# A decoder layer on one core: the squares of two norms summed by VectorE instead of TensorE, and the low parts of two tiles ahead of the samples

## The chip, the cores and the metric

One Trainium2 chip, one of its cores. The metric is the device time of one execution in microseconds (us), lower is better. The times of the kernel before are 2039.47, 2039.68 and 2043.07 us, median 2039.68.

## What is computed

One inference step of a hybrid decoder layer for 256 prompt tokens and 8 samples of 4 tokens, 288 columns in all, in float32, model width 2048. The parts that the change touches are the norm between the two sub-layers and the final norm:

```python
def _rmsnorm(x, g):
    xf = x.astype(jnp.float32)
    y = xf * lax.rsqrt(jnp.mean(xf * xf, axis=-1, keepdims=True) + NORM_EPS)
    return (y * g.astype(jnp.float32)).astype(x.dtype)
...
    x = x + gt1 * jnp.dot(mix, p["w_o"])

    h2 = _rmsnorm(x, p["g_norm2"]) * (1.0 + sc2) + sh2
    u, ffn_buf_new = _causal_dwconv(jnp.dot(h2, p["w_up"]), ffn_buf, p["w_ffn_conv"])
    u_gate, u_val = jnp.split(u + p["b_ffn_conv"], 2, axis=-1)
    x = x + gt2 * jnp.dot(jax.nn.silu(u_gate) * u_val, p["w_down"])
...
    y_prompt = _rmsnorm(h_p, g_final)
    y_sample = _rmsnorm(h_s, g_final)
```

## The kernel before

Everything is kept feature-major: x is 16 tiles (KT) of 128 features by 288 columns (256 of the prompt, SEQ, then 32 of the samples, NS). The weights come from memory as one stream of slots of 512 KB, each four tiles of input features (KS) by two tiles of output features (CT), into eight buffers raw_a and on. For float32 accuracy each slot is split: ScalarE rounds it into a high part (L740, hi_a to hi_c, a ring of four), GpSimd subtracts to get the rest (L700, written beside or over the raw slot). TensorE then does 24 matmuls of 288 columns for a slot: for each of 4 x 2 weight tiles high x high (L2150), high x low of the activation (L2151), and behind them, when the rest is there, rest x high (L2155). The names hi, lo and rest are these parts.

The order of the work on every engine is written out by hand; engines wait for each other through counters (semaphores), and each engine executes its own list in order.

A product runs in groups: a group is one pair of output tiles, 4 slots in the w_o product (phase "wo", 8 groups, three sets of two PSUM banks) and 3 slots in the last of three down products (phase "dn2", 8 groups, two sets of banks). Behind each group VectorE adds the gated result to two tiles of x (residual, L2003 to L2010) and raises x_done or down_done; ScalarE squares the two tiles into the two halves of sq (squares_of, L751), for which it waits until sq_used says that the halves are free. It does that at places in its own list between weight conversions. TensorE sums a square over the 128 features of a tile with a matmul against a matrix of ones into bank 7 (norm_part, L2182). The profile shows each such float32 matmul as two. In the w_o product the sums of group g-1 are issued behind group g; in the last down product behind the second slot of group m (the hook within=). The sums of the last pair follow alone, in both norms, and then norm_end raises ssq_ready; ScalarE turns bank 7 into the reciprocal root (rms, L757 and L759).

After the norm in the middle, second_norm on VectorE and tiles_round on ScalarE produce h tile by tile. For the prompt columns of tile k VectorE scales x into a bank (L1371), ScalarE rounds it into h_hi (L789), and VectorE forms the low part h_lo (second_lo, L1356), two tiles later in its list. The sample columns go in two bunches, tiles 0 to 3 (ka) and 4 to 15 (kb): scaled and shifted by VectorE (second_samples, L1343 and L1346), rounded by ScalarE (L787), low part by VectorE (second_lo_samples, L1351). TensorE's first group of the up product waits for the low part of each tile in turn, and for the low samples of ka before its first slot and of kb before its second. The change in the diff's second part moves the calls for kb within second_norm's loop over k.

After the last norm VectorE scales all 16 tiles of x (L2092), and the output is stored.

Of the kernel before, what the change touches and what calls it, by code (L numbers as in the profile page):

```python
# [17 lines left out]
P = 128  # L18
# [8 lines left out]
N = SEQ + NS  # L27
NC = 1 + DB
NCP = NC + NC % 2
KT = D_MODEL // P  # L30
KS, CT = 4, 2
# [128 lines left out]
SUPERS = ((0, 4), (4, 4), (8, 3))  # L160
# [88 lines left out]
def decoder_step(nc, A, O):  # L249
    f32, f32r, i32 = mybir.dt.float32, mybir.dt.float32r, mybir.dt.int32  # L250
    ALU, ACT, AX = mybir.AluOpType, mybir.ActivationFunctionType, mybir.AxisListType
    ds = bass.ds
    ctx = ExitStack()
    with ctx:
# [23 lines left out]
        ident, ones = cv["ident"], cv["ones"]  # L278
# [103 lines left out]
        np_ = Place(rows_at)  # L382
        sq = np_.take("sq", [P, 2, N])
        ht_at = np_.at
        hs = Place(ht_at).take("hs", [P, KT, NS])
        np_.at += 4 * HB * N
        hf = np_.take("hf", [P, HB, SEQ])
        amul = np_.take("amul", [P, KT, NC])

# [73 lines left out]
        bank = [ctx.enter_context(nc.psum_tensor(f"bank{i}", [P, 512], f32)) for i in range(8)]  # L463
# [3 lines left out]
        def sem(name):  # L467
            return ctx.enter_context(nc.semaphore(name))
# [13 lines left out]
        sq_ready, sq_used, ssq_ready, rs_ready = sem("sq_ready"), sem("sq_used"), sem("ssq_ready"), sem("rs_ready")  # L482
        xr_ready, sq_sum = sem("xr_ready"), sem("sq_sum")
# [35 lines left out]
        def grp(name, sets, g, i=0, per=0):  # L519

            return g % sets, gbase[name][g % sets] + g // sets + i * (per // sets)
# [9 lines left out]
        def raw_at(name, j, i=0, per=0):  # L531

            s_ = BASE[name] + j
            first, _, size, before = next(t for t in stretches if t[0] <= s_ < t[1])
            return (s_ - first) % size, before[(s_ - first) % size] + (s_ - first) // size + i * (per // size)

        def wait_group(eng, name, g, i=0, per=0):

            if name == "go":
                j, per_j = 2 * g + 1, 2 * per  # L540
            elif name[:2] == "dn":
                k = SUPERS[int(name[2])][1]
                j, per_j = k * g + k - 1, k * per
            else:
                j, per_j = 4 * g + 3, 4 * per
            r, use = raw_at(name, j, i, per_j)
            eng.wait_ge(raw_free[r], use + 2)
# [693 lines left out]
        def _(dve):  # L1241
            V = nc.vector
            T_, S_, STT, CP = V.tensor_tensor, V.tensor_scalar, V.scalar_tensor_tensor, V.tensor_copy
# [97 lines left out]
            def second_samples(ks, count):  # L1341

                T_(hs_p[:, ks, :], hs[:, ks, :], bank[7][:, SEQ:N].unsqueeze(1).to_broadcast([P, count, NS]), ALU.mult)  # L1343
                dve.drain()
                sh = ada[:, 3 * KT + ks.start:3 * KT + ks.stop, 1:NC].unsqueeze(2).to_broadcast([P, count, TS, DB])
                T_(tb16(hs_p[:, ks, :]), tb16(hs_p[:, ks, :]), sh, ALU.add).then_inc(hs_t, 1)  # L1346

            def second_lo_samples(ks, n):

                dve.wait_ge(hs_hi, n)  # L1350
                T_(h_lo[:, ks, SEQ:], hs_p[:, ks, :], h_hi[:, ks, SEQ:].bitcast(f32), ALU.subtract).then_inc(hs_lo, 1)  # L1351
# [7 lines left out]
            def second_norm():  # L1359

                ka, kb = slice(0, 4), slice(4, KT)
                T_(tb16(hs[:, :, :]), tb16(x[:, :, SEQ:]), of_b16(amul[:, :, 1:NC]), ALU.mult)
                dve.drain()
                dve.wait_ge(rs_ready, 2)
                second_samples(ka, 4)
                for k in range(KT):
                    if k >= 2:
                        second_lo(k - 2)
                    if k >= 3:
                        dve.wait_ge(h_lo_ready, KT + HB + k - 2)  # L1370
                    STT(bank[4 + k % 3][:, 0:SEQ], x[:, k, 0:SEQ], amul[:, k, 0:1], bank[7][:, 0:SEQ], ALU.mult, ALU.mult).then_inc(h_t, 1)  # L1371
                    if k == 1:
                        second_lo_samples(ka, 5)
                        second_samples(kb, KT - 4)
                    if k == 3:
                        second_lo_samples(kb, 6)
                second_lo(KT - 2)
                second_lo(KT - 1)
# [68 lines left out]
            def iqm_half(u):  # L1447
# [3 lines left out]
                for same in (1, 0):  # L1451
# [7 lines left out]
            sets = [(sc_p[:, 0:P], wk_p[:, 0:P], top8[:, 0, :]), (sc_p[:, P:], wk_p[:, P:], top8[:, 1, :]),  # L1459
                    (sc_s[:, :], wk_s[:, :], top8[:, 2, :])]  # L1460
# [537 lines left out]
            def residual(bs, t, gate_tile):  # L1998
# [11 lines left out]
                    T_(xt[:, SEQ:], xt[:, SEQ:], bank[2 * bs + c][:, SEQ:N], ALU.add)  # L2010
                dve.drain()

            dve.wait_ge(hist_in, 16)
            h_old, h_new = hcx[:, :, 0:DB], hcx[:, :, DB:HI_F]
            wf = lambda w_: vec[:, V_WF + w_ * 2 * FT:V_WF + (w_ + 1) * 2 * FT].unsqueeze(2).to_broadcast([P, 2 * FT, DB])
# [5 lines left out]
            second_scale()  # L2021
            for g in range(KT // CT):
                bs, _ = grp("wo", 3, g)
                wait_group(dve, "wo", g)
                if g % (KT // CT // 2) == 0:
                    dve.wait_ge(x_back[g // (KT // CT // 2)], 16)
                residual(bs, 2 * g, 2 * KT)
                dve.sem_inc(grp_free[bs], 1)
                dve.sem_inc(x_done, 2)
# [48 lines left out]
            for n, (first, count) in enumerate(SUPERS):  # L2078
                with dve.Fori(0, count) as i:
                    for half in range(2):  # L2080
                        up_pair(f"up{n}", half, first, i)
                for m in range(KT // CT):
                    bs, _ = grp(f"dn{n}", 2, m)
                    wait_group(dve, f"dn{n}", m)
                    residual(bs, 2 * m, 5 * KT)
                    dve.sem_inc(grp_free[bs], 1)
                    dve.sem_inc(down_done, 1)
# [8 lines left out]
        def _(pe):  # L2096
            MM = nc.tensor.matmul
# [60 lines left out]
                            ins.then_inc(ring_free, 1)  # L2158
                ins.then_inc(raw_free[r], 1)

            def group(name, sets, g, j0, nslots, hi_t, lo_t, i=0, per_g=0, per_j=0, norm=None, chunk=None, mixed=False, within=None):

                bs, cnt = grp(name, sets, g, i, per_g)
                banks = (bank[2 * bs], bank[2 * bs + 1])
                pe.wait_ge(grp_free[bs], cnt + 1)
                for s_ in range(nslots):
                    if norm is not None and s_ < 2:
                        pe.wait_ge(hs_lo, 5 + s_)
                    if mixed:
                        pe.wait_ge(mix_done, 2 * s_ + 2)  # L2170
                    if chunk is not None:
                        pe.wait_ge(act_ready, 2 * (chunk + s_) + 2)
                    slot(name, j0 + s_, lambda k: hi_t(s_ * KS + k), lambda k: lo_t(s_ * KS + k), banks,
                         s_ == 0, s_ == nslots - 1, i, per_j, None if norm is None else norm * KT + HB + s_ * KS)
                    if within is not None and s_ == 1:
                        within()

            hh, hl = (lambda k: h_hi[:, k, :]), (lambda k: h_lo[:, k, :])

            def norm_part(n, s_):  # L2180
                pe.wait_ge(sq_ready, 4 + (n - 1) * KT + s_ + 1)
                MM(bank[7][:, 0:N], ones, sq[:, s_ % 2, :], start=(s_ == 0), stop=(s_ == KT - 1)).then_inc(sq_used, 1)  # L2182

            def norm_end(n):
                pe.wait_ge(sq_used, n * KT + 2)
# [435 lines left out]

            for g in range(KT // CT):
                group("wo", 3, g, 4 * g, 4, mh, ml, mixed=g == 0)
                for s_ in range(CT * g - CT, CT * g):
                    if s_ >= 0:
                        norm_part(1, s_)
            for s_ in range(KT - CT, KT):
                norm_part(1, s_)
            norm_end(1)
# [1 line left out]
            ah, al = (lambda k: act_hi[:, k, :]), (lambda k: act_lo[:, k, :])  # L2631
            for n, (first, count) in enumerate(SUPERS):
                up, dn = f"up{n}", f"dn{n}"
                if n == 0:
                    for g in range(4):
                        group(up, 2, g, 4 * g, 4, hh, hl, norm=None if g else 1)
                peel = 1 if n == 0 else 0
                with pe.Fori(0, count - peel) as i:
                    for g in range(4):
                        group(up, 2, g + 4 * peel, 4 * g + 16 * peel, 4, hh, hl, i, 4, 16)  # L2640
                if n < len(SUPERS) - 1:
                    with pe.Fori(0, KT // CT // 2) as i:
                        for m in range(2):
                            group(dn, 2, m, count * m, count, ah, al, i, 2, 2 * count, chunk=first)
                else:
                    for m in range(KT // CT):
                        def sums(m=m):
                            for s_ in range(CT * m - CT, CT * m):
                                norm_part(2, s_)
                        group(dn, 2, m, count * m, count, ah, al, chunk=first, within=sums if m else None)  # L2650
            for s_ in range(KT - CT, KT):
                norm_part(2, s_)
            norm_end(2)
# [112 lines left out]
```

## Time and profile before

| | |
|---|---|
| median of three runs | 2039.68 us (2039.47 to 2043.07) |
| the profiled execution, its own time | 2045.23 us |
| its span | 2043.4 us |
| w_o product with its norm sums | about 1071 to 1169 us of the span |
| h of the second norm, TensorE at half clock | about 1172 to 1182 |
| three up and down products | 1175 to 2027.5 |
| last down product with its norm sums | about 1944 to 2031 |
| last scaling and store | 2033 to the end |

The profile is one execution. Its page gives busy times and the span in 40 slices; the views of the trace used below are the busy time of each engine in chosen windows with the granted clock of TensorE (1.00 is 2.4 GHz, 0.50 is 1.2 GHz), the chain of work that ended last in order of time, the timeline of one engine, and the instructions of one tile. Matmuls overlap: one of 288 columns shows as 0.29 us, but they start 0.13 us apart, so starts are what is to be compared.

### The profile page before, as it was taken

What the parts mean: (1) busy time and instruction counts of PE and PEld (TensorE: products, weight loads), DVE (VectorE), ACT (ScalarE), POOL (GpSimd) and SP (SyncE); (2) the same over time, 40 slices, a digit from 0 to 9 for tenths busy, and PEclk for the clock granted to TensorE, in tenths of its full rate; (3) what the DMA queues carried; (4) which work ended last, traced back from release to release, by engine and by line L of the source; (5) the groups of instructions that cost most, each with busy time, mean ns of one, the idle gap of its engine ahead of it and who ended that gap; (6) DMA issues with size and microseconds to landing.
All of it is one profiled execution on the core that took longest, in us unless ns stands there. A gap on an engine that the chain in (4) does not pass through costs nothing.

```text
span 2043.4 us, 38282 instructions
## 1 busy us (share of the span) xinstructions
PE 1957.9 (96%) x15132; PEld 1835.6 (90%) x15132; DVE 619.1 (30%) x1722; ACT 827.2 (40%) x1365; POOL 1179.4 (58%) x496
## 2 busy tenths in 40 slices
PE   6899989999989989999899899999999999999997
PEld 2399989998878878888799899999999999999996
DVE  1347534443214233232251142221122221122212
ACT  1353436643214232242443455553344443344432
POOL 0176646663424334333587667777777777777763
PEclk9699999999999999999999999999999999999998
DMA  9966434444868877888874444444544445444442
GB/s 393 411 213 196 136 104 142 149 163 126 227 206 245 251 238 232 248 244 247 260 224 159 138 144 166 164 164 165 164 166 165 167 166 168 166 165 165 164 161 77
DMA packets 177856, 390.77 MB, mean 191 GB/s; under 512 B 27522, under 2 KB 101698, under 8 KB 177090
## 3 DMA queue, kind: packets, MB, share of 16 engines
q1 hardware_dynamic: 156592, 370.11, 55.6%
q10 hardware_dynamic: 21138, 18.90, 2.9%
q8 instruction: 89, 1.46, 0.3%
q14 instruction: 37, 0.30, 0.0%
HBM read 380.01 MB, written 8.88 MB: 190 GB/s over the span
## 4 chain that ended last, share of the span: by engine, by line
PE 87%; DMA 7%; ACT 2%; DVE 2%; issue 1%; DVEq 0%; ACTq 0%; POOL 0%; SPq 0%; PEldq 0%; POOLq 0%
PE bank L2150 25%; PE bank L2151 25%; PE bank L2155 24%; DMA raw_a<-in_stream 4%; PE bank L2126 2%; DMA raw_c<-in_stream 1%; PE bank L2487 1%; PE bank L2495 1%; PE bank L2498 1%; DMA raw_b<-in_stream 1%; PE bank L2591 1%; PE bank L2182 1%; PE bank L2570 1%; PE bank L2102 1%; PE bank L2115 1%
## 5 line engine op out<-in xcount | busy, mean ns | idle before, releaser
L700 POOL TENSOR_TENSOR rest_a<-raw_a,hi_a 128x1024 fp32r<-128x1024 f32 x185 | 442.5, 2394 | 460.5 <-ACT hi_a L740 460.5
L2150 PE MATMUL bank<-h_hi,hi_a 128*128 128x288 f32 x1752 | 488.1, 304 | 6.7 <-ACT hi_a L740 5.6
L2151 PE MATMUL bank<-h_lo,hi_a 128*128 128x288 f32 x1752 | 477.0, 298 | 0.0
L2150 PEld LDWEIGHTS bank<-h_hi,hi_a 128*128 128x128 f32 x1752 | 334.2, 191 | 23.1 <-issue 13.7
L740 ACT ACTIVATE hi_a<-raw_a 128x1024 fp32r<-128x1024 f32 x185 | 195.9, 1059 | 371.0 <-PE bank L2155 230.8
L2151 PEld LDWEIGHTS bank<-h_lo,hi_a 128*128 128x128 f32 x1752 | 334.9, 191 | 0.4
L2155 PE MATMUL bank<-h_hi,rest_a 128*128 128x288 f32 x1600 | 245.6, 296 | 0.1
L2155 PEld LDWEIGHTS bank<-h_hi,rest_a 128*128 128x128 f32 x1600 | 224.8, 190 | 0.3 <-POOL rest_a L700 0.3
L700 POOL TENSOR_TENSOR rest_b<-raw_b,hi_a 128x1024 fp32r<-128x1024 f32 x67 | 161.4, 2409 | 100.5 <-ACT hi_a L740 100.5
L700 POOL TENSOR_TENSOR rest_a<-raw_a,hi_b 128x1024 fp32r<-128x1024 f32 x56 | 134.6, 2404 | 64.6 <-ACT hi_b L740 64.6
L2150 PE MATMUL bank<-h_hi,hi_b 128*128 128x288 f32 x616 | 167.9, 299 | 0.0
L2151 PE MATMUL bank<-h_lo,hi_b 128*128 128x288 f32 x616 | 165.6, 295 | 0.0
L740 ACT ACTIVATE hi_a<-raw_b 128x1024 fp32r<-128x1024 f32 x67 | 70.9, 1059 | 140.2 <-PE bank L2155 102.4
L2003 DVE SCALAR_TENSOR_TENSOR x<-bank,ada,x 128x256 f32<-128x256 f32 x64 | 28.0, 480 | 316.9 <-PE bank L2155 316.7
L700 POOL TENSOR_TENSOR rest_b<-raw_b,hi_c 128x1024 fp32r<-128x1024 f32 x39 | 93.5, 2397 | 45.9 <-ACT hi_c L740 45.9
L2150 PEld LDWEIGHTS bank<-h_hi,hi_b 128*128 128x128 f32 x616 | 115.6, 188 | 0.8 <-ACT hi_a L740 0.3
L2151 PEld LDWEIGHTS bank<-h_lo,hi_b 128*128 128x128 f32 x616 | 116.0, 188 | 0.3
L700 POOL TENSOR_TENSOR rest_a<-raw_a,hi_c 128x1024 fp32r<-128x1024 f32 x39 | 93.4, 2396 | 35.2 <-ACT hi_c L740 35.2
L700 POOL TENSOR_TENSOR rest_c<-raw_c,hi_a 128x1024 fp32r<-128x1024 f32 x39 | 94.0, 2410 | 31.3 <-ACT hi_a L740 31.2
L700 POOL TENSOR_TENSOR rest_c<-raw_c,hi_b 128x1024 fp32r<-128x1024 f32 x39 | 93.8, 2406 | 29.9 <-ACT hi_b L740 29.9
L2155 PE MATMUL bank<-h_hi,rest_b 128*128 128x288 f32 x696 | 106.7, 296 | 0.1
L740 ACT ACTIVATE hi_b<-raw_a 128x1024 fp32r<-128x1024 f32 x56 | 59.4, 1060 | 110.1 <-PE bank L2155 108.9
(486 smaller groups left out, 3960.2 us busy)
## 6 DMA issues: line engine op xcount, KB each, us to landing
raw_a<-in_stream SPq DMA_DIRECT2D x396, 512.0 KB, 3.7
raw_b<-in_stream SPq DMA_DIRECT2D x160, 512.0 KB, 3.3
raw_c<-in_stream SPq DMA_DIRECT2D x94, 512.0 KB, 3.3
raw_m<-in_stream SPq DMA_DIRECT2D x34, 512.0 KB, 6.5
st<-in_state ACTq DMA_DIRECT2D x16, 512.0 KB, 7.0
out_state_s<-st ACTq DMA_DIRECT2D x8, 512.0 KB, 6.3
x<-in_x SPq DMA_DIRECT2D x2, 1152.0 KB, 13.7
x<-in_x ACTq DMA_DIRECT2D x2, 1152.0 KB, 6.6
```

The source lines that it names most:

```text
L700: nc.gpsimd.tensor_tensor(rest_in(name, r), raw_of(name, r), w_hi[q].bitcast(f32), ALU.subtract).then_inc(lo_ready, 1)
L740: A_(w_hi[q], raw_of(name, r), ACT.Copy).then_inc(hi_ready, 1)
L2003: STT(xt[:, 0:SEQ], bank[2 * bs + c][:, 0:SEQ], gt[:, 0:1], xt[:, 0:SEQ], ALU.mult, ALU.add)
L2102: return nc.tensor.transpose(out, in_, ident[0:n, 0:n])
L2115: last = MM(bank[2 * (n % 2)][32 * k:32 * k + NCP, 0:CT * P], c_f[:, s_ * KS + k, :], raw[r][:, k, :], start=(s_ == 0), stop=(s_ == KT // ...
L2126: last = MM(bank[2][32 * q:32 * q + NCP, 0:CT * P], c_f[:, k, :], raw_m[r][:, q, :], start=(k == 0), stop=(k == KT - 1))
L2150: MM(banks[c][:, 0:N], w_, hi_of(k), start=(first and k == 0), stop=False)
L2151: ins = MM(banks[c][:, 0:N], w_, lo_of(k), start=False, stop=False)
L2155: ins = MM(banks[c][:, 0:N], rest_in(name, r)[:, k, c * P:(c + 1) * P], hi_of(k), start=False, stop=(last_ and k == KS - 1))
L2182: MM(bank[7][:, 0:N], ones, sq[:, s_ % 2, :], start=(s_ == 0), stop=(s_ == KT - 1)).then_inc(sq_used, 1)
L2487: ins = MM(blk(3, ch), bt[:, l % 2, ch, :], tt[:, 4 + ch, :], start=True, stop=True)
L2495: ins = MM(blk(4, ch), x_p[:, ch, :], tt[:, ch, :], start=True, stop=True)
```

## The change

Seven of the eight pairs of squares in each of the two norms are no longer summed by TensorE one by one. VectorE copies the first pair (two tiles, 128x576) into a new buffer sq_acc and adds the next six to it, each ahead of the residual of the following group, and raises sq_used itself. TensorE sums the two halves of sq_acc with two matmuls behind the last group, and the last pair as before. The hook within= goes. sq_acc lies over a buffer (hf) that only the first norm uses.

In second_norm the samples of tiles 4 to 15 are scaled after k = 3 instead of after k = 1, and their low part comes after k = 5 instead of after k = 3. The low parts of tiles 0 and 1 are thereby ahead of them in VectorE's list.

```diff
+        sq_acc = Place(np_.at).take("sq_acc", [P, 2, N])
         hf = np_.take("hf", [P, HB, SEQ])
...
                     if k == 1:
                         second_lo_samples(ka, 5)
+                    if k == 3:
                         second_samples(kb, KT - 4)
-                    if k == 3:
+                    if k == 5:
                         second_lo_samples(kb, 6)
...
+            def gather_squares(n, g):
+
+                dve.wait_ge(sq_ready, 4 + (n - 1) * KT + 2 * g + 2)
+                if g == 0:
+                    CP(sq_acc[:, :, :], sq[:, :, :]).then_inc(sq_sum, 1)
+                else:
+                    dve.wait_ge(sq_sum, 4 + (n - 1) * (KT // CT - 1) + g)
+                    T_(sq_acc[:, :, :], sq_acc[:, :, :], sq[:, :, :], ALU.add).then_inc(sq_sum, 1)
+                dve.wait_ge(sq_sum, 4 + (n - 1) * (KT // CT - 1) + g + 1)
+                dve.sem_inc(sq_used, 2)
...
             for g in range(KT // CT):
                 bs, _ = grp("wo", 3, g)
+                if g:
+                    gather_squares(1, g - 1)
                 wait_group(dve, "wo", g)
...
                     bs, _ = grp(f"dn{n}", 2, m)
+                    if n == len(SUPERS) - 1 and m:
+                        gather_squares(2, m - 1)
                     wait_group(dve, f"dn{n}", m)
...
-                    if within is not None and s_ == 1:
-                        within()
...
-                MM(bank[7][:, 0:N], ones, sq[:, s_ % 2, :], start=(s_ == 0), stop=(s_ == KT - 1)).then_inc(sq_used, 1)
+                MM(bank[7][:, 0:N], ones, sq[:, s_ % 2, :], start=False, stop=(s_ == KT - 1)).then_inc(sq_used, 1)
+
+            def gathered_part(n):
+
+                pe.wait_ge(sq_sum, 4 + n * (KT // CT - 1))
+                for c in range(2):
+                    MM(bank[7][:, 0:N], ones, sq_acc[:, c, :], start=(c == 0), stop=False)
...
                 group("wo", 3, g, 4 * g, 4, mh, ml, mixed=g == 0)
-                for s_ in range(CT * g - CT, CT * g):
-                    if s_ >= 0:
-                        norm_part(1, s_)
+            gathered_part(1)
             for s_ in range(KT - CT, KT):
                 norm_part(1, s_)
...
-                        def sums(m=m):
-                            for s_ in range(CT * m - CT, CT * m):
-                                norm_part(2, s_)
-                        group(dn, 2, m, count * m, count, ah, al, chunk=first, within=sums if m else None)
+                        group(dn, 2, m, count * m, count, ah, al, chunk=first)
+            gathered_part(2)
             for s_ in range(KT - CT, KT):
                 norm_part(2, s_)
```

## Rows read from the trace of the kernel before

**Rows 1.** The page: busy us of each engine; TensorE's clock in 40 slices.
```profile
PE 1957.9 (96%) x15132; PEld 1835.6 (90%) x15132; DVE 619.1 (30%) x1722; ACT 827.2 (40%) x1365; POOL 1179.4 (58%) x496
...
PEclk9699999999999999999999999999999999999998
```

**Rows 2.** Windows: length, busy us (instructions) by engine, clock, DMA share, GB/s.
```profile
1100.00:1165.00 65.00, 65.00 (x479) 64.16 (x478) 5.46 (x24) 25.06 (x31) 45.21 (x20) 1.00 0.46 155
...
1954.00:2027.00 73.00, 73.00 (x530) 71.52 (x529) 9.48 (x42) 24.50 (x33) 42.68 (x18) 1.00 0.34 113
```

**Rows 3.** The chain in the w_o product: start us, length us, what.
```profile
1083.82 0.97 PE bank L2182 x4
...
1100.60 1.07 PE bank L2155 x8
1103.79 1.07 PE bank L2155 x8
...
1152.29 0.97 PE bank L2182 x4
```

**Rows 4.** The same chain in the last down product.
```profile
2002.35 0.97 PE bank L2182 x4
...
2023.38 0.97 PE bank L2182 x4
```

**Rows 5.** Timeline at both norms' ends: start, length, engine, line, operation [idle before].
```profile
1165.82 1.13 PE L2182 MATMUL bank<-sq,consts 128*128 128x288 f32 x4
1168.11 1.24 PE L2182 MATMUL bank<-sq,consts 128*128 128x288 f32 x4 [1.16 <-ACT sq L751]
...
2029.68 1.24 PE L2182 MATMUL bank<-sq,consts 128*128 128x288 f32 x4 [2.14 <-ACT sq L751]
...
1153.92 0.78 ACT L751 ACTIVATE sq<-x 128x288 f32<-128x288 f32 x2 [1.39 <-DVEq L2028]
...
1167.61 0.78 ACT L751 ACTIVATE sq<-x 128x288 f32<-128x288 f32 x2 [4.57 <-DVEq L2028]
```

**Rows 6.** Timeline after norm 1: TensorE, VectorE, ScalarE.
```profile
1175.01 0.58 PE L2150 MATMUL bank<-h_hi,hi_c 128*128 128x288 f32 x1 [5.66 <-DVE h_lo L1356]
...
1177.97 0.61 PE L2150 MATMUL bank<-h_hi,hi_c 128*128 128x288 f32 x1 [0.70 <-DVE h_lo L1356]
...
1180.06 2.12 PE L2155 MATMUL bank<-h_hi,rest_a 128*128 128x288 f32 x8
1181.98 0.39 PE L2150 MATMUL bank<-h_hi,hi_a 128*128 128x288 f32 x1
...
1173.29 0.55 DVE L1343 TENSOR_TENSOR bank<-hs,bank 128x384 f32<-128x384 f32 x1
...
1174.39 0.47 DVE L1356 SCALAR_TENSOR_TENSOR h_lo<-bank,ada,h_hi 128x256 fp32r<-128x256 f32 x1
...
1176.96 0.56 DVE L1351 TENSOR_TENSOR h_lo<-bank,h_hi 128x384 fp32r<-128x384 f32 x1 [0.92 <-ACT h_hi L787]
...
1172.82 0.87 ACT L789 ACTIVATE h_hi<-bank,ada 128x256 fp32r<-128x256 f32 x2
```

**Rows 7.** Windows of 2 us after norm 1, columns as in rows 2.
```profile
1171.00:1173.00 2.00, 0.00 (x0) 0.00 (x0) 1.20 (x4) 1.99 (x5) 0.27 (x1) 0.74 0.02 4
...
1181.00:1183.00 2.00, 2.00 (x12) 2.00 (x12) 2.00 (x7) 1.11 (x3) 0.00 (x0) 0.70 0.03 8
```

**Rows 8.** Timeline of VectorE, GpSimd, ScalarE; an addition of two tiles (duration ns min/median/max).
```profile
1062.03 3.10 DVE L2016 TENSOR_TENSOR htmp<-hcx,vec 128x704 f32<-128x704 f32 x1 [0.21 <-issue]
...
1065.10 3.10 POOL L700 TENSOR_TENSOR rest_b<-raw_b,hi_a 128x1024 fp32r<-128x1024 f32 x1 [0.72 <-ACT hi_a L740]
...
1094.66 2.40 POOL L700 TENSOR_TENSOR rest_c<-raw_c,hi_a 128x1024 fp32r<-128x1024 f32 x1 [0.79 <-ACT hi_a L740]
...
1094.48 0.76 ACT L751 ACTIVATE sq<-x 128x288 f32<-128x288 f32 x2
...
L1269 DVE TENSOR_TENSOR sq<-sq x4: 749/750/753, 25.8 to 43.6; 128x576 f32<-128x576 f32 x4
```

More of the change, by code:

```diff
@@ L2159, in slot, with group @@
                 ins.then_inc(raw_free[r], 1)
-            def group(name, sets, g, j0, nslots, hi_t, lo_t, i=0, per_g=0, per_j=0, norm=None, chunk=None, mixed=False, within=None):
+            def group(name, sets, g, j0, nslots, hi_t, lo_t, i=0, per_g=0, per_j=0, norm=None, chunk=None, mixed=False):
                 bs, cnt = grp(name, sets, g, i, per_g)
```

## The prediction

> **What bounds the kernel now.** I read the page first: TensorE is busy for 96% of the span, the next engine, GpSimd, for 58%, and TensorE's clock is at its full level of 2.4 GHz in nearly every slice [rows 1]. Then the windows over the two stages that the change touches. In the w_o product TensorE has no idle microsecond in 65 at a granted clock of 1.00, while GpSimd is busy 45.2 of 65, ScalarE 25.1 and VectorE 5.5; in the last down product it is busy 73 of 73 and the others far less [rows 2]. So in both stages whatever TensorE issues is paid in full, and whatever VectorE does is free as long as nobody waits for it.
>
> Then the chain of waits, which runs through TensorE alone there. A slot of weights (24 matmuls) repeats every 3.19 us: the eight rest matmuls start at 1100.60 and again at 1103.79 [rows 3]. Between the groups sits a piece "L2182 x4 0.97": one pair of norm sums, where each source matmul shows as two [rows 3, 4]. The group pitch says the same: L2182 comes every 13.69 us (1083.82 to 1152.29 in five groups), which is four slots of 3.18 and 0.97.
>
> **Pairs removed.** Each norm had eight pairs. In the w_o stage seven come after groups 1 to 7. The first six are on the path (1083.8 to 1152.3). The seventh starts at 1165.82, when TensorE has no matmul of its own left and waits for the last residual anyway: even so it idles 1.16 us before the eighth [rows 5]. That one was free. In the last down product all seven sit inside a group, behind its second slot, and the chain shows 0.97 for each (2002.35 and 2023.38 are two of them) [rows 4]. So 6 x 0.97 + 7 x 0.97 = 12.6 us leave the path. Nothing takes their place at once: TensorE's next work is a slot whose weights are ready. In a slot's 3.19 us GpSimd needs 2.40 (the row at 1094.66) [rows 8], and both products run from rings that are four slots deep.
>
> **The gathered part.** Two source matmuls, four in the trace, as long as one pair: 1.13 us. It is issued behind the last group. In norm 1 it stands exactly where the free seventh pair stood, 1165.82, with 1.16 us of idle time left behind it [rows 5]. In norm 2 TensorE is idle for 2.14 us before the last pair [rows 5], so 1.13 fits, with 1.0 to spare. It waits for VectorE's seventh addition; that needs the squares of pair 6, which ScalarE writes at 1153.92, 12 us before [rows 5]. Taken: 0. If this cover were gone it would cost 0.97 per norm, 1.9 in all.
>
> **VectorE's work.** Per norm one copy and six additions of 128x576 f32. The nearest row is 750 ns for an addition of that shape; the trace has no copy of two tiles, and it is bounded by 0 and by that 0.75, since it reads one operand where the addition reads two; hidden either way. Each stands ahead of a residual, in a stretch in which VectorE idles (5.5 us busy of 65) [rows 2, 8]. The new wait: the residual of group g is queued behind the squares of pair g-1. They are written at 1094.48 to 1095.24 while group g ends at 1097.5 (13.69 behind 1083.82) [rows 3, 8], so some 2.3 us are left for 0.75. What waits for that residual is the bank of a later group and ScalarE's squares, a group later; only the last residual of each norm is on the path, and its gather was possible 12 us before. The counters that ScalarE waits for before it overwrites sq are now raised by VectorE ahead of the residual, earlier than by TensorE. Taken: 0.
>
> **A rule that speaks against it.** The rows at the start of the w_o stage show a collision: a VectorE operation on two SBUF operands that meets GpSimd's subtraction takes 3.10 us, and the next subtraction itself 3.10 instead of 2.40 [rows 8]. The Trainium skill, "SBUF — State Buffer", section "Who interferes with whom", says why: an instruction of VectorE with two SBUF inputs takes the read interface that GpSimd also reads by, and whoever comes second waits for the whole of the other's instruction. By that rule every gather in the w_o stage collides (the squares come at 1095.2, GpSimd runs 1094.66 to 1097.06), and the trace agrees that such collisions happen.
>
> In rows: a gather then starts when the subtraction ends, 1097.06, and is over at about 1097.85, so that this group's residual starts 0.3 us late. That residual has a whole group of slack. GpSimd loses up to 0.7 us once in four slots, and has 0.8 spare in each. So the sum stays; the rival below has the case in which it doesn't.
>
> **The order in the second norm.** After norm 1 TensorE waits for the low parts of h, tile by tile. Before: VectorE scales the samples of tiles 4 to 15 (1173.29 to 1174.39, 1.10 us) ahead of the low part of tile 0 (1174.39); TensorE starts 0.62 later, at 1175.01, does tiles 0 and 1 (8 matmuls take 2.09 from a restart, as 1177.97 to 1180.06 shows) and stops, because VectorE waited 0.92 for ScalarE's rounding of those samples; it goes on at 1177.97 [rows 6]. After: low part 0 comes as soon as ScalarE has rounded tile 0 (its two roundings start at 1172.82 and take 0.87), at about 1173.35; then, at 0.39 a step, scale 2, low part 1, scale 3 (1174.52), the samples at 1174.91, low part 2 at 1176.01. TensorE starts at 1173.97 and restarts at about 1176.63: 1.3 us ahead of before. The 0.92 us wait goes too, since ScalarE rounds the samples while VectorE does low part 2, scale 4 and low part 3. ScalarE itself now waits for the samples with tiles 4 to 15 queued behind; they reach it at 1176.0, and low part 4 is wanted only at 1178.0. Slot 1 needs tiles 4 to 7 from 1180.7 on; at 0.78 a tile they are done by 1180.9, ahead of each one's turn. In real time all of this lies 5.8 us earlier.
>
> The clock takes part of it. It falls to 0.50, the 1.2 GHz level, at about 1171.96 after TensorE has stood still (0.74 granted in 1171 to 1173), and is back at 1182.2 (0.70 in 1181 to 1183) [rows 7]. If it rises as long after the last restart as before (4.2 us), that is 1180.8, and 1.2 us are gained. If it rises as long after its fall as before, slot 1 runs 1.5 us at half speed, half of it is lost again, and 0.5 is gained. Bounds: 0.2 if it rises a microsecond later still, 1.9 if it rises inside slot 0. Taken: 0.9.
>
> **The sum.** 12.6 + 0.9 = 13.5 us. The profiled execution has a span of 2043.4 and a time of 2045.23; it would become 2029.9 and 2031.7. It lies 5.5 above the median of the runs, 2039.68, whose own spread is 2039.47 to 2043.07; nothing in the sum depends on which execution it is, so from the median: 2039.68 - 13.5 = **2026.2**.
>
> **Rivals.**
> 1. *The collision reaches the path.* If the gather of pair 6 met a GpSimd operation or waited for ScalarE so long that the last residual started late, each norm would pay up to 3.15 us (2.40 and 0.75), 6.3 in all: 2032.5. Against it: 12 us of room and a GpSimd that has run out of work in both tails. Chance 0.06.
> 2. *The gathered part is not covered,* or the reordering gives nothing: 0.9 to 2.8 us less, 2027 to 2029. Chance 0.12.
> 3. *The matmuls removed were only a filler.* If the weights arrived no faster than before, TensorE would wait where the pair stood, and only the reordering would be left: 2038.8, no change that can be told. For it: nothing but that the streams are dense. Against it: slots without a pair run at 3.19 us with GpSimd idle a quarter of the time, and no wait of TensorE stands in either stage. Chance 0.04.
> 4. *Slower: TensorE waits for banks in the last down product.* It has two sets of banks there, so group m+2 needs residual m within the 9.5 us of group m+1. Residual m now stands behind the gather, that behind ScalarE's squares, and those behind a weight conversion which itself waits for TensorE's slots. A residual takes 1.6 (from the last group's end, about 1166.0, to its squares at 1167.61 [rows 5]), so a delay over 7.9 us stalls TensorE, once in each of six groups; from 7.9 + 13.5/6 = about 10.2 us of delay the kernel is slower than before, at 11.5 us it takes 2026.2 + 6 x 3.6 = 2047.8. For it: the waits do form such a ring. Against it: in the stage before the squares are written 2.3 us ahead of the group's end, and the conversion that they follow waits only for the group's first slot. Chance 0.02.
> 5. *The change doesn't do what it says* (pairs still issued one by one, or the sum started twice): the L2182 rows would still be 32 in each norm, time unchanged. The diff leaves one pair and the gathered two: 0.01.
>
> Chances: forecast 0.75. Less than 0.2% (4.1 us) can't be told from no change; faster 0.94, same 0.04, slower 0.02. The range: from 2039.5 - 12.6 - 1.9 = 2025.0, and a little below for a gain that I haven't seen, up to 2029 for rival 2 and one more for the runs' own spread: 2023.5 to 2030.
>
> **What would show it.** Group pitch in the w_o stage down from 13.69 to 12.7 and in the last down product from 10.52 to 9.55, with TensorE busy throughout; 4 matmuls each of the gathered part and of the norm sum per norm; TensorE's idle time before the last pair of norm 2 down from 2.14 to about 1; gathers of 0.75 us, or up to 3.1 beside GpSimd; the first matmul on h 5.8 us after the start of norm 1's last pair instead of 6.9, and the stop behind tile 1 shorter. Wrong would be: residuals that start more than a microsecond after their group, new TensorE waits for VectorE, or a half clock that lasts past the second slot.

## The result, and the profile after

The changed kernel takes 2027.19 us in the median of five runs (2022.84 to 2029.96) against 2039.47 (2037.59 to 2043.07); the ratio is 0.9928 with a 95% interval of 0.9909 to 0.9947, 14.7 us less (10.8 to 18.6). The two medians by themselves lie 12.3 us apart. A second comparison, run among the experiments, gives 0.9918 (0.9896 to 0.9939). The forecast was 2026.2 and 13.5 us less.

The profiled execution has a span of 2021.0, which is 22.4 us less than the span of before. That is more than the change does: this execution is the fastest of its five, and the one of before is slower than all five of its runs. The page first: VectorE's busy time is up by 29.5 us, TensorE's down by 19.6.

```profile
PE 1938.3 (96%) x15084; PEld 1820.8 (90%) x15084; DVE 648.6 (32%) x1736; ACT 827.5 (41%) x1365; POOL 1179.8 (58%) x496
...
PEclk7799999999989999999999999999999999999998
```

Windows over the two stages (columns as in rows 2). TensorE is as full as before; VectorE's share in the w_o product has gone from 8% [rows 2] to 30%.

```profile
1090.00:1152.00 62.00, 62.00 (x471) 62.00 (x470) 18.76 (x36) 26.13 (x32) 46.28 (x20) 1.00 0.50 167
1935.00:2004.00 69.00, 68.92 (x521) 68.92 (x522) 24.25 (x49) 25.57 (x34) 44.05 (x19) 1.00 0.37 124
```

The chain of waits in the w_o product, against rows 3: no piece of sums between the groups, and every slot is 3.17 to 3.18 us long. Before, the slots behind a pair were 3.18 to 3.19.

```profile
1087.11 1.05 PE bank L2172 x8
1090.29 1.05 PE bank L2172 x8
1093.46 1.05 PE bank L2172 x8
...
1153.75 1.06 PE bank L2172 x8
```

TensorE's timeline at both ends of the norms, against rows 5: the gathered part (L2203) and the last pair (L2197). TensorE idles 1.17 us between them in both norms; before it was 1.16 in norm 1 and 2.14 in norm 2. So the gathered part is covered in both.

```profile
1154.64 1.13 PE L2203 MATMUL bank<-sq_acc,consts 128*128 128x288 f32 x4
1156.94 1.24 PE L2197 MATMUL bank<-sq,consts 128*128 128x288 f32 x4 [1.17 <-ACT sq L752]
...
2004.99 1.13 PE L2203 MATMUL bank<-sq_acc,consts 128*128 128x288 f32 x4
2007.30 1.24 PE L2197 MATMUL bank<-sq,consts 128*128 128x288 f32 x4 [1.17 <-ACT sq L752]
```

The gathers, timeline of ScalarE, VectorE and GpSimd in the w_o product and then in the last down product, against rows 8. The squares are ready at 1089.07, and VectorE's addition starts at once by the profile; but it lasts 2.40 instead of 0.76, and ends 0.62 behind the end of GpSimd's subtraction (1090.88). GpSimd's next subtraction starts after 0.77 us of idle time, as without a collision, and takes 2.40. The residual follows at 1091.64, 0.3 us behind the group's end at 1091.34 (the rest matmuls of 1090.29 and 1.05).

```profile
1088.31 0.76 ACT L752 ACTIVATE sq<-x 128x288 f32<-128x288 f32 x2
...
1089.10 2.40 DVE L2022 TENSOR_TENSOR sq_acc<-sq_acc,sq 128x576 f32<-128x576 f32 x1 [8.98 <-ACT sq L752]
1091.64 0.88 DVE L2005 SCALAR_TENSOR_TENSOR x<-bank,ada,x 128x256 f32<-128x256 f32 x2
...
1088.48 2.40 POOL L701 TENSOR_TENSOR rest_c<-raw_c,hi_a 128x1024 fp32r<-128x1024 f32 x1 [0.77 <-ACT hi_a L741]
1091.66 2.40 POOL L701 TENSOR_TENSOR rest_c<-raw_c,hi_b 128x1024 fp32r<-128x1024 f32 x1 [0.77 <-ACT hi_b L741]
...
1961.67 2.40 DVE L2022 TENSOR_TENSOR sq_acc<-sq_acc,sq 128x576 f32<-128x576 f32 x1 [2.63 <-ACT sq L752]
...
1961.05 2.40 POOL L701 TENSOR_TENSOR rest_b<-raw_b,hi_a 128x1024 fp32r<-128x1024 f32 x1 [0.77 <-ACT hi_a L741]
```

The restart after norm 1, timeline of TensorE and VectorE, against rows 6. Counted from the start of norm 1's last pair (1168.11 before, 1156.94 after), TensorE's first matmul on h comes at 5.85 us instead of 6.90, its second start at 8.43 instead of 9.86, and the rest matmuls of slot 1 at 13.44 instead of 16.08 (1184.19 in the kernel before, whose line comes first).

```profile
1184.19 1.23 PE L2155 MATMUL bank<-h_hi,rest_a 128*128 128x288 f32 x8
```

```profile
1162.79 0.58 PE L2167 MATMUL bank<-h_hi,hi_c 128*128 128x288 f32 x1 [4.61 <-DVE h_lo L1357]
...
1165.37 0.61 PE L2167 MATMUL bank<-h_hi,hi_c 128*128 128x288 f32 x1 [0.32 <-DVE h_lo L1357]
...
1166.94 1.23 PE L2172 MATMUL bank<-h_hi,rest_a 128*128 128x288 f32 x8
...
1170.38 1.23 PE L2172 MATMUL bank<-h_hi,rest_a 128*128 128x288 f32 x8
...
1162.16 0.48 DVE L1357 SCALAR_TENSOR_TENSOR h_lo<-bank,ada,h_hi 128x256 fp32r<-128x256 f32 x1
...
1163.73 0.56 DVE L1344 TENSOR_TENSOR bank<-hs,bank 128x384 f32<-128x384 f32 x1
...
1164.84 0.47 DVE L1357 SCALAR_TENSOR_TENSOR h_lo<-bank,ada,h_hi 128x256 fp32r<-128x256 f32 x1
...
1166.40 0.55 DVE L1352 TENSOR_TENSOR h_lo<-bank,h_hi 128x384 fp32r<-128x384 f32 x1
```

TensorE's clock there, in windows (columns as in rows 2, clock third from the end): a grant of 0.93 in the last window puts its return to the full 2.4 GHz at about 1166.3, inside slot 0, 0.9 us behind the second start. In rows 7 it rose 4.2 us behind it.

```profile
1160.00:1162.00 2.00, 0.00 (x0) 0.00 (x0) 1.37 (x5) 1.99 (x5) 0.43 (x1) 0.50 0.01 4
...
1164.00:1166.00 2.00, 1.68 (x7) 1.33 (x6) 1.93 (x5) 1.08 (x3) 0.00 (x0) 0.50 0.00 0
1166.00:1168.00 2.00, 2.00 (x15) 2.00 (x15) 2.00 (x6) 0.92 (x3) 0.00 (x0) 0.93 0.00 0
```

### The profile page after: what moved, and what is told of

Read it like the earlier page. It is cut to its first block, busy times and chain, and to the rows that moved or that the text cites. A ratio compares the mean times of both kernels' runs of the same rounds, so it can differ in the third digit from the quotient of the medians.

```text
span 2021.0 us, 38226 instructions
## 1 busy us (share of the span) xinstructions
PE 1938.3 (96%) x15084; PEld 1820.8 (90%) x15084; DVE 648.6 (32%) x1736; ACT 827.5 (41%) x1365; POOL 1179.8 (58%) x496
## 4 chain that ended last, share of the span: by engine, by line
PE 88%; DMA 6%; ACT 2%; DVE 2%; issue 1%; DVEq 1%; ACTq 0%; POOL 0%; SPq 0%; PEldq 0%; POOLq 0%
PE bank L2167 25%; PE bank L2168 25%; PE bank L2172 25%; DMA raw_a<-in_stream 3%; PE bank L2143 2%; PE bank L2508 1%; PE bank L2516 1%; PE bank L2519 1%; DMA raw_b<-in_stream 1%; DMA raw_c<-in_stream 1%; PE bank L2612 1%; PE bank L2132 1%; PE bank L2591 1%; PE bank L2119 1%; PE bank L2327 0%
## 5 line engine op out<-in xcount | busy, mean ns | idle before, releaser
L2167 PEld LDWEIGHTS bank<-h_hi,hi_a 128*128 128x128 f32 x1752 | 332.5, 190 | 23.0 <-issue 12.8
L2167 PE MATMUL bank<-h_hi,hi_c 128*128 128x288 f32 x352 | 95.9, 298 | 4.9 <-DVE h_lo L1357 4.9
## 6 DMA issues: line engine op xcount, KB each, us to landing
x<-in_x SPq DMA_DIRECT2D x2, 1152.0 KB, 13.7
```

Source lines behind the costliest of these rows:

```text
L2167: MM(banks[c][:, 0:N], w_, hi_of(k), start=(first and k == 0), stop=False)
```

## Experiments

Every run left a trace, so five distances can be read off thirteen executions. All are starts: of residual 1 in the w_o product (the end of group 1), from there to norm 1's last pair, from that pair to the rest matmuls of slot 1, from the first matmul after TensorE's wait at the head of the last down product to that product's first residual, and from that residual to norm 2's last pair.

| kernel | residual 1 | to last pair 1 | to slot 1's rest | head of down | to last pair 2 |
|---|---|---|---|---|---|
| before | 1083.86 | 84.25 | 16.08 | 5.02 | 75.76 |
| before, again (e4) | 1077.11 | 84.26 | 16.40 | 3.48 | 75.73 |
| order only (e2) | 1081.08 | 84.26 | 14.58 | 5.01 | 75.74 |
| pairs twice (e6) | 1078.52 | 90.01 | 16.37 | 3.48 | 82.45 |
| gather only (e1) | 1081.81 | 78.26 | 16.85 | 3.48 | 68.75 |
| after | 1078.68 | 78.26 | 13.44 | 3.48 | 68.74 |
| after, again (e3) | 1077.30 | 78.26 | 14.28 | 5.02 | 68.75 |
| no additions (e5) | 1080.29 | 78.25 | 14.42 | 5.03 | 68.74 |
| delay of 7 (e7) | 1089.37 | 78.26 | 14.16 | 5.01 | 70.49 |
| delay of 14 (e8) | 1079.62 | 78.26 | 13.44 | 3.47 | 104.29 |
| spare matmuls (e9) | 1076.90 | 78.26 | 13.44 | 3.49 | 68.77 |
| split samples (e10) | 1082.80 | 78.26 | 13.48 | 3.49 | 68.76 |
| both (e11) | 1077.36 | 78.26 | 13.47 | 5.01 | 68.74 |

**e1, the gather alone.** The changed kernel with the old order in the second norm:

```diff
                     if k == 1:
                         second_lo_samples(ka, 5)
-                    if k == 3:
                         second_samples(kb, KT - 4)
-                    if k == 5:
+                    if k == 3:
                         second_lo_samples(kb, 6)
```

> The change with the old order in the second norm. Theory (the pairs on the path are the gain): the group pitch in the w_o product is 12.69 us as in the changed kernel, in the last down product 9.52; six pairs and seven pairs at 1.00 us each, 13.0 us less than before in the median, and the restart after norm 1 as before, 13 to 15 us from the start of the last pair to slot 2 less 3.2. Rival (half of the gain is the order): 6 to 8 us less than before.

Measured: ratio 0.9933 (0.9912 to 0.9955), 2027.76 us in the median against 2043.14. Both products have the distances of the changed kernel, and the restart that of the old order. Its lines in TensorE's timeline, and the clock in a window 7 us behind the first start:

```profile
1166.97 0.58 PE L2166 MATMUL bank<-h_hi,hi_c 128*128 128x288 f32 x1 [5.66 <-DVE h_lo L1357]
1169.93 0.61 PE L2166 MATMUL bank<-h_hi,hi_c 128*128 128x288 f32 x1 [0.70 <-DVE h_lo L1357]
1172.02 2.12 PE L2171 MATMUL bank<-h_hi,rest_a 128*128 128x288 f32 x8
1176.92 1.23 PE L2171 MATMUL bank<-h_hi,rest_a 128*128 128x288 f32 x8
```

```profile
1174.00:1176.00 2.00, 2.00 (x11) 2.00 (x11) 2.00 (x6) 1.16 (x3) 0.00 (x0) 0.53 0.42 125
```

So the gather carries 13.0 of the gain: 84.25 - 78.26 = 6.0 and 75.76 - 68.75 = 7.0.

**e2, the order alone.** The other half, put into the kernel before:

```diff
                     if k == 1:
                         second_lo_samples(ka, 5)
+                    if k == 3:
                         second_samples(kb, KT - 4)
-                    if k == 3:
+                    if k == 5:
                         second_lo_samples(kb, 6)
```

> The kernel before with the new order in the second norm alone. Theory: the low part of tile 0 starts 1.2 us earlier, TensorE's first matmul on h comes 5.8 us after the start of the last pair instead of 6.9, and the start of slot 2 (17.2 us after it before, 14.5 in the changed kernel) between 14.5 and 16.2 us after it, depending on when the clock rises; 0.5 to 2.6 us less in time, too little for the median to show. Rival (the order gives nothing, the restart is set by the clock): slot 2 at 17 us as before.

Measured: ratio 0.9984 (0.9968 to 1.0000), an interval that ends at no change; 3.3 us less at its middle. In the trace both starts are where they are in the changed kernel, 5.85 and 8.42 us behind the last pair (1165.34), though the clock rose later there (slot 2 starts at 15.6 us):

```profile
1171.19 0.58 PE L2151 MATMUL bank<-h_hi,hi_c 128*128 128x288 f32 x1 [4.61 <-DVE h_lo L1356]
1173.76 0.61 PE L2151 MATMUL bank<-h_hi,hi_c 128*128 128x288 f32 x1 [0.32 <-DVE h_lo L1356]
```

**e3 and e4, both kernels once more,** without an edit.

> The changed kernel once more. Theory: 13.5 to 15 us less than before in the same call; of the 22.4 us between the two profiled spans, the 5.2 before the w_o product and the 1.6 of a half clock in the last down product are one execution's and don't come again: the spread of the time at which group 1 of the w_o product ends is several us over executions. Rival (the change also speeds up the stages ahead of it): group 1 ends at 1078.7 again, 5 us earlier than in every kernel with pairs.

> The kernel before once more, for its trace alone. Theory: the group pitch is 13.69 and 10.52 to 0.02 us, the distance from the start of the last pair to slot 2 is 16 to 18 us, and the end of group 1 of the w_o product moves by microseconds against 1083.8. Rival: it stays at 1083.8 within 1 us, and the changed kernel's 1078.7 is the change's doing.

Measured: e3 has the ratio 0.9918 (0.9896 to 0.9939), 2024.37 us in the median; e4 was a single execution, 2037.35 us. The end of group 1 lies at 1077.11 in e4, a kernel with pairs, 6.8 us from where it lay in the first trace of the same program, and between 1076.9 and 1089.4 over all thirteen. The 5.2 us ahead of the w_o product were one execution's, and so were 1.5 at the head of the last down product. There TensorE waits 1.86 us in every trace, and in six of thirteen (before, e2, e3, e5, e7 and e11) the clock falls afterwards. Two windows show it, the first of the kernel before and the second of the changed one; the half clock costs 1.54 us (5.02 against 3.48).

```profile
1950.00:1952.00 2.00, 2.00 (x11) 2.00 (x10) 0.00 (x0) 0.00 (x0) 0.00 (x0) 0.55 0.00 0
```

```profile
1935.00:1937.00 2.00, 1.92 (x14) 1.93 (x15) 0.00 (x0) 0.00 (x0) 0.83 (x1) 1.00 0.42 170
```

The expectation for e3 said that this 1.6 would not come again; it did, in e3 itself. With that the 22.4 us between the two profiled spans come apart without a rest: 5.2 ahead of the w_o product, 6.0 in it, 2.6 in the restart, 1.5 from the clock, 7.0 in the last down product.

**e5, no additions.** VectorE sets sq_acc to ones once per norm and otherwise only raises the counters, so the kernel leaves 14 of the 16 squares out of each norm's sum:

```diff
                 if g == 0:
-                    CP(sq_acc[:, :, :], sq[:, :, :]).then_inc(sq_sum, 1)
+                    V.memset(sq_acc[:, :, :], 1.0).then_inc(sq_sum, 1)
                 else:
-                    dve.wait_ge(sq_sum, 4 + (n - 1) * (KT // CT - 1) + g)
-                    T_(sq_acc[:, :, :], sq_acc[:, :, :], sq[:, :, :], ALU.add).then_inc(sq_sum, 1)
+                    dve.sem_inc(sq_sum, 1)
```

> The changed kernel without VectorE's copy and additions: sq_acc is set to ones once per norm and only the counters are raised, so the sums of 14 tiles are left out of both norms. Theory (VectorE's work is covered even where it collides with GpSimd): same pitches, 12.69 and 9.52, same time as the changed kernel to 1 us. Rival (the collisions cost something): up to 2 us less.

Measured: ratio 0.9925 (0.9905 to 0.9944), and 78.25 and 68.74 us, equal to the changed kernel to 0.01. VectorE's additions, stretched to 2.4 us or not, cost nothing.

**e6, pairs twice.** In the kernel before, every pair but the last is issued a second time:

```diff
                 pe.wait_ge(sq_ready, 4 + (n - 1) * KT + s_ + 1)
+                if s_ < KT - CT:
+                    MM(bank[6][:, 0:N], ones, sq[:, s_ % 2, :], start=True, stop=True)
                 MM(bank[7][:, 0:N], ones, sq[:, s_ % 2, :], start=(s_ == 0), stop=(s_ == KT - 1)).then_inc(sq_used, 1)
```

> The kernel before with each pair of sums but the last issued twice, the second time into an unused bank. Theory (a pair on the path costs 1.00 us, one behind the last w_o group nothing): pitch 14.69 in the w_o product and 11.52 in the last down product, 13.0 us slower than before; the seventh pair of norm 1 stands in 1.16 us of idle time and takes 1.0 of it. Rival (the pairs fill waits for weights): pitches unchanged, no slower.

Measured: ratio 1.0069 (1.0049 to 1.0089), 14.1 us slower. The distances grow by 5.76 and 6.70, that is 0.96 for each of six and seven pairs. Taking a pair away gives 1.00, so 0.03 to 0.04 lie in the slots that follow a break and are lost once per break; a break of twice the length loses no more. The seventh pair of norm 1 is covered as computed: both copies are issued from 1166.24 on, and of 1.16 us idle 0.19 are left.

```profile
1166.24 0.65 PE L2183 MATMUL bank<-sq,consts 128*128 128x288 f32 x2
1166.72 0.65 PE L2184 MATMUL bank<-sq,consts 128*128 128x288 f32 x2
...
1168.53 1.24 PE L2184 MATMUL bank<-sq,consts 128*128 128x288 f32 x4 [0.19 <-ACT sq L751]
```

**e7 and e8, a delay ahead of each residual.** The changed kernel with 7 or 14 operations on an unused bank:

```diff
                     if n == len(SUPERS) - 1 and m:
                         gather_squares(2, m - 1)
+                        for _ in range(7):
+                            S_(bank[6][:, 0:512], bank[6][:, 0:512], 1.0, None, ALU.mult)
+                            dve.drain()
```

> The changed kernel with seven dependent operations on VectorE (128x512 in PSUM, estimated 0.7 us each, some 5 us) between the gather and the residual of each group from 1 on in the last down product. VectorE idles 3.05 us there, so the residual comes about 2 us late. Theory of the loop (gather, delay, residual, squares must fit in one group of 9.52 us; they take 3 to 3.5 without the delay): no loss, pitch 9.52. Theory of the prediction's fourth rival (only banks bind, from 7.9 us): no loss either.

> The same with fourteen operations, some 10 us. Theory of the loop: 10 and 3.3 exceed 9.52 by 3.8, and each group from the third on comes about that much later, so the last residual starts some 20 us late and the kernel takes 20 to 30 us longer. Theory of the fourth rival's price (delay less 7.9 in each of six groups): 12 us longer. Theory that VectorE's work there is free: no loss.

Measured in the traces, since the times of single runs (2038.28 and 2060.37) hold the spread of the stages ahead (1089.37 in e7). Seven operations take 5.35 us and cost 1.75, not nothing: the inner residuals come 2.5 us late without harm, but the last one stands directly on the path, and comes as early as residual 6, squares, gather and delay allow. Fourteen take 10.78 and cost 35.5, more than any of the three theories said. VectorE's timeline of e8 shows the loop: a residual at 1970.85, squares, an addition at 1973.27, the delay, the next residual at 1985.03. A turn takes 14.17, of which 3.39 are not the delay. Six turns are 4.65 too long each, 27.9 us, and the first residual of the loop (1956.65) came 7.6 late; the two make up the 35.5.

```profile
1970.85 0.88 DVE L2005 SCALAR_TENSOR_TENSOR x<-bank,ada,x 128x256 f32<-128x256 f32 x2
...
1973.27 0.76 DVE L2022 TENSOR_TENSOR sq_acc<-sq_acc,sq 128x576 f32<-128x576 f32 x1 [0.98 <-ACT sq L752]
1974.18 10.78 DVE L2102 TENSOR_SCALAR bank<-bank 128x512 f32<-128x512 f32 x14
1985.03 0.88 DVE L2005 SCALAR_TENSOR_TENSOR x<-bank,ada,x 128x256 f32<-128x256 f32 x2
```

**e9, e10 and e11, what is left of the restart.** e9 adds spare matmuls behind norm 1's last pair; e10 splits the samples of tiles 4 to 15 in two bunches (ScalarE's and TensorE's waits follow); e11 has both.

```diff
             norm_end(1)
+            for _ in range(9):
+                MM(bank[3][:, 0:N], ones, sq[:, 0, :], start=True, stop=True)
```

```diff
-                ka, kb = slice(0, 4), slice(4, KT)
+                ka, kb, kc = slice(0, 4), slice(4, 8), slice(8, KT)
...
                     if k == 3:
-                        second_samples(kb, KT - 4)
+                        second_samples(kb, 4)
                     if k == 5:
                         second_lo_samples(kb, 6)
+                    if k == 7:
+                        second_samples(kc, KT - 8)
+                    if k == 9:
+                        second_lo_samples(kc, 7)
```

> The changed kernel with nine spare float32 matmuls of ones on sq into an unused bank behind norm 1's last pair, some 4.4 us of TensorE's 4.6 idle. From the start of the last pair to the rest matmuls of slot 1 the changed kernel takes 13.4 to 14.6 us over six executions, with a half clock for 7 to 9 us of it. Theory (activity keeps the clock): the granted clock stays at 1.00, slot 0 runs at the full clock, and what bounds is VectorE's low parts: slot 1's rest at 13.0 to 13.3 us; 0.5 to 1.3 us less in time. Rival (the clock falls anyway, or the spare matmuls run late): 14 us or more.

> The changed kernel with the samples of tiles 4 to 15 in two bunches, 4 to 7 after k = 3 (low part after k = 5) and 8 to 15 after k = 7 (after k = 9). Theory (VectorE's block ahead of low part 2 sets TensorE's second start): the block shrinks from 1.1 to some 0.7 us, the second start comes 0.3 to 0.4 us earlier (8.4 us after the start of the last pair now), and the wait for tile 7 in slot 1 is gone; the rest of slot 1 at 13.0 to 14.2 us. Rival: TensorE is busy with tiles 0 and 1 at half clock until 7.9 us anyway, and nothing shows.

> Both together. Theory: low parts are the only bound once the clock stays up, so the earlier low parts 2 to 7 pay in full: rest of slot 1 at 12.3 to 12.8 us, 1 to 2 us less time than the changed kernel, too little to tell in the median. Rival: as with the spare matmuls alone.

Measured: ratios 0.9933 (0.9918 to 0.9947), 0.9931 (0.9917 to 0.9945) and 0.9935 (0.9920 to 0.9949); none can be told from the changed kernel. The spare matmuls do keep the clock: in e9 it is at 1.00 in every window through the restart, and TensorE now waits 1.08 us for low part 2.

```profile
1159.16:1161.16 2.00, 2.00 (x10) 1.40 (x9) 2.00 (x6) 1.57 (x4) 1.38 (x1) 1.00 0.00 0
1161.16:1163.16 2.00, 1.34 (x8) 0.95 (x8) 1.93 (x6) 0.95 (x2) 1.00 (x1) 1.00 0.00 0
1163.16:1165.16 2.00, 1.57 (x10) 1.35 (x11) 2.00 (x6) 1.38 (x3) 0.00 (x0) 1.00 0.00 0
```

Slot 1's rest then comes at 13.44 us, which two executions of the new order (after and e8) reached without them; the other four with the new order stand at 14.16 to 14.58. So 13.44, a little above the 13.0 to 13.3 that I expected, is set by VectorE's low parts, and the clock costs up to 1.1 us more. Splitting the samples gives back what it takes. In e11 slot 0's rest comes at 9.30 us instead of e9's 9.86, but then the second bunch, which is scaled after k = 7, stands ahead of low part 6 in VectorE's list, and TensorE stops for 0.46 us in slot 1 (below):

```profile
1166.31 0.42 DVE L1344 TENSOR_TENSOR bank<-hs,bank 128x256 f32<-128x256 f32 x1
1166.80 0.43 DVE L1347 TENSOR_TENSOR bank<-bank,ada 128x256 f32<-128x256 f32 x1
1167.14 0.48 DVE L1357 SCALAR_TENSOR_TENSOR h_lo<-bank,ada,h_hi 128x256 fp32r<-128x256 f32 x1
...
1167.68 0.41 PE L2171 MATMUL bank<-h_hi,hi_a 128*128 128x288 f32 x1 [0.46 <-DVE h_lo L1357]
```

So e10 and e11 reach slot 1's rest at 13.48 and 13.47, although in e10 the stop behind tile 1 is gone and tile 2 starts at 7.90 instead of 8.43. The low part of that bunch stands ahead of low part 8, and slot 2's rest comes at 16.94 and 16.95 against 16.64 in the changed kernel. My 12.3 to 12.8 for e11 missed the first of these.

## Why the prediction was right, point by point

**Pairs removed: 12.6 forecast, 13.0 measured.** The count was right (six and seven on the path, the seventh of norm 1 free), and e1 and e6 show it from both sides. A pair was mis-sized by 0.03: I took its own 0.97 and left out that the slots behind it run 3.18 to 3.19 instead of 3.17 [rows 3].

**The gathered part: 0, and 0.** Rival 2's first half (up to 1.9) fell; 1.17 us of idle time are left behind it in norm 2 where I had 1.0.

**VectorE's work: 0, and 0** (e5). The collision was forecast for the w_o product alone, and it happens in both: ten of twelve additions take 2.40 us, and both copies about 2 (2.10 and 1.96). So my bound of 0.75 for the copy fell: it reads one operand, which the prediction's rule for two does not cover, and yet both times it ended 0.3 us behind GpSimd's subtraction. It is hidden too. No run shows the copy beside an idle GpSimd. The reason is the same in both, and I had the row for one [rows 8]: ScalarE writes squares right behind a weight conversion, and the same conversion releases GpSimd. GpSimd, which I let pay up to 0.7 us, pays nothing, since the gather always came second and ended within GpSimd's own 0.77 us of idle time. Where VectorE came first GpSimd paid: in the kernel before, an operation of VectorE had begun at 1065.05 (below), and the subtraction at 1065.10 took 3.10 [rows 8]. That whoever comes second pays the whole wait is the rule of the Trainium skill that the prediction weighed, and both traces agree with it.

```profile
1065.05 0.88 DVE L2017 TENSOR_TENSOR hcx<-hcx,vec 128x704 f32<-128x704 f32 x1
```

**The order: 0.9 forecast, 2.4 measured,** the step whose size was off. The old order stands at 16.1 to 16.9 us over four executions (mean 16.4), the new one at 13.4 to 14.6 over six (mean 14.05). VectorE's part was close: the second start moved by 1.44, and I had 1.3. What failed is "the clock takes part of it". I took its rise as 4.2 us behind the last start or 10.2 behind its fall; in the granted clock of the traces it rose 9.3 to 12.5 us behind the last pair with the new order (after, e2, e3, e5, e7 and e8) and 14.1 to 15.8 with the old one (before, e1 and e4). It moved by more than TensorE's starts did, and so gave about 1 us on top instead of taking 0.1 to 0.8. My upper bound of 1.9 was too low.

The fall, read from the granted clock in windows of 1 us, does not follow the order: it came 1.9 to 5.0 us behind the last pair, early or late in both orders. What differs is how long the half clock then lasted. Where it fell at 3.8 or later, that was 10.2 us with the old order (before, e4, e6) and 6.8 with the new one (e3, e7). Where it fell at 1.9 to 2.3, it was 13.7 with the old (e1) and 10.2 with the new (e2, e5). In the two that fell at 2.5 and 2.7 (after, e8) it was 6.8. So at like falls the half clock is shorter with the new order, on few executions. My case of the same 10.2 us behind the fall held in two of six, and that of 4.2 us behind the last start in one (e2, 4.1; the others 0.9 to 3.7). Why it is shorter is open. That the stop between tiles 1 and 2 is 0.32 instead of 0.70 us is argued, not shown: after a stop of 0.32 the half clock lasted 6.8 as well as 10.2, and in e10, which has no stop there, 6.8.

**The sum.** By the distances, 6.0 + 7.0 + 2.4 = 15.4 us. The two comparisons say 14.7 and 16.8 at their middles, with intervals some 8 us wide. So 13.5 was low by 2, of which 0.4 are pairs and 1.5 the restart. That the median came out 1.0 us from 2026.2, and above it, is luck within the spread: the runs of one kernel lie 7 us apart.

**The rivals.** Rival 3 (only a filler) fell by e1 and e6, rival 5 by the trace, and rival 2's second half (the order gives nothing) by the restart's 2.4. Rival 1 fell: the collision is everywhere but in the last gather of each norm (0.76 us, GpSimd at rest), which is the only one that it was about. Rival 4 did not occur in the changed kernel, where every turn of the last down product took 9.52 us. Its mechanism was not the one that binds either: banks do stop TensorE in e8 (4.35 us ahead of 1972.38), but what sets the pace is VectorE's and ScalarE's own loop, 3.39 us and the delay. It is saturated at 9.52 - 3.39 = 6.1 us of delay, not 7.9, and then every group pays. At 10.78 us my price gives (10.78 - 7.9) x 6 = 17; e8 cost 35.5.

## What to carry to other kernels

On a full TensorE a cross-partition sum by matmul is paid even if nobody waits for it. Add on VectorE first and let TensorE sum once, and put that once where it waits anyway: pairs that already stand in such a place bring nothing. When work is put ahead of a step on an idle engine, look at the last turn, which has no slack behind it, and at the loop through the other engines, which saturates earlier than the buffers. Judge a change of 0.7% by distances within the trace: those over the two products repeat to 0.04 us, while the stages ahead moved by 12 us between executions.

## What I had not expected of the hardware

A wait of 1.86 us at the head of the last down product was followed by a half clock in six of thirteen executions and not in the other seven, with the same instructions; it costs 1.54 us. After the idle time of 4.6 or 5.7 us the clock fell in every execution without spare matmuls (eleven), and came back 3.5 to 6.6 us behind TensorE's first start with the new order, 7.2 to 8.9 with the old one. TensorE's full clock survived that stretch in both executions that filled it with 4.4 us of spare matmuls (e9 and e11).

The Trainium skill, "TensorE: Matmul & The Clock Gate", section "Why this matters for your kernels", warns of idle gaps between bursts of matmuls, but of longer ones than this. The traces agree for the gaps of 4.6 and 5.7 us, and disagree for the short one, where the half clock followed a stop of 1.86 us in six of thirteen.
